# Second expert matrix of a hybrid-attention MoE backbone: loaded by partition halves in 8 KB runs instead of by column halves in 4 KB runs

## What is computed

```python
D_MODEL = 1024; N_GROUPS = 4; EXPERTS_PER_GROUP = 8      # 32 experts
TOP_K = 2; D_EXPERT = 256
# moe_w1, moe_w3: (DEPTH, 32, 1024, 256)    moe_w2: (DEPTH, 32, 256, 1024)

def hierarchical_moe(t, wg, bg, we, be, w1, w3, w2):
    ...                     # top-1 group, top-2 experts in it: combine (n, 32)
    def add_expert(acc, p):
        w1_e, w3_e, w2_e, c_e = p
        hidden = jax.nn.silu(t @ w1_e) * (t @ w3_e)
        return acc + c_e[:, None] * (hidden @ w2_e), None
    y, _ = lax.scan(add_expert, jnp.zeros_like(t), (w1, w3, w2, combine.T.astype(t.dtype)))
    return y
```

## Time and profile before

| what | value |
|---|---|
| time, median of 3 runs | 1144.73 us (1143.92 to 1146.38) |
| the profiled execution's own time | 1142.64 us |
| its span, first to last instruction | 1140.6 us |
| TensorE matmul busy | 976.4 us (86%) |
| VectorE, ScalarE, GpSimd busy | 29%, 23%, 21% |
| expert stage of layer 0 on TensorE, U and Dn | 365.2 to 635.3 us |
| expert stage of layer 1 on TensorE, U and Dn | about 858 to 1116.7 us |
| mean granted TensorE clock | 0.938 of 2.4 GHz |
| moved by DMA | 312.66 MB, mean 274 GB/s |

### The profile page before, as it was taken

The page is one execution under the profiler, slowest core; times in us unless marked ns, Lnnn a source line. Parts: engine busy times, 40 slices in busy tenths (PEclk is TensorE's granted clock), DMA queues, the critical chain, the costliest instruction groups (busy, mean ns, idle before and its releaser), DMA issues.

```text
span 1140.6 us, 17923 instructions
## 1 busy us (share of the span) xinstructions
PE 976.4 (86%) x5993; PEld 640.8 (56%) x5994; DVE 333.8 (29%) x720; ACT 259.5 (23%) x539; POOL 235.7 (21%) x331
## 2 busy tenths in 40 slices
PE   3999998989996998888998399999959989878881
PEld 2444475457884555555555175878845555555550
DVE  2169953542165110000100361255170101000103
ACT  3111023452131221111221230223122212111212
POOL 1118010100123132323231100000123323223310
PEclk9999999999997998998998799999978989998986
DMA  9992235994259799999999793232054999999972
GB/s 370 289 315 74 74 88 207 380 352 184 74 175 342 262 402 406 408 408 406 356 408 400 268 348 114 74 111 89 23 203 151 399 404 387 409 405 405 403 281 111
DMA packets 126899, 312.66 MB, mean 274 GB/s; under 512 B 28567, under 2 KB 59543, under 8 KB 126068
## 3 DMA queue, kind: packets, MB, share of 16 engines
q1 hardware_dynamic: 101488, 285.63, 66.5%
q10 hardware_dynamic: 14628, 13.53, 3.8%
q0 software_dynamic: 10720, 12.64, 3.2%
HBM read 312.49 MB, written 21.76 MB: 293 GB/s over the span
## 4 chain that ended last, share of the span: by engine, by line
PE 59%; DMA 26%; DVE 6%; ACT 3%; SPq 2%; issue 2%; ACTq 1%; POOL 0%; POOLq 0%; DVEq 0%
DMA ring<-in_moe_w 22%; PE ps L700 17%; PE ps L814 12%; PE ps L840 5%; PE ps L710 5%; PE ps L1005 4%; PE ps L636 3%; PE ps L1130 2%; SPq L572 2%; PE ps L667 1%; DMA PR<-in_odd_conv 1%; PE ps L792 1%; PE ps L683 1%; PE ps L729 1%; DMA RT<-pair_out 1%
## 5 line engine op out<-in xcount | busy, mean ns | idle before, releaser
L814 PE MATMUL ps<-ring,RT 128*64 128x256 f32 x2144 | 280.8, 420 | 59.7 <-DMA ring<-in_moe_w 56.7
L814 PEld LDWEIGHTS ps<-ring,RT 128*64 128x64 f32 x2144 | 186.1, 152 | 132.3 <-issue 68.2
L700 PE MATMUL ps<-RT,ring 128*128 128x512 f32 (+1 forms) x576 | 196.1, 500 | 1.0 <-ACT RT L1382 1.0
L700 PEld LDWEIGHTS ps<-RT,ring 128*128 128x128 f32 x576 | 109.4, 192 | 84.9 <-issue 76.6
L840 PE MATMUL ps<-ring,RT 128*64 128x512 f32 x536 | 127.8, 593 | 1.9 <-DVE RT L1771 1.1
L1754 DVE TENSOR_TENSOR RT<-RT,ps 64x256 f32<-64x256 f32 x64 | 27.0, 423 | 337.8 <-ACT RT L1332 337.8
L1332 ACT ACTIVATE RT<-ps 64x256 f32<-64x256 f32 x64 | 24.2, 378 | 300.1 <-PE ps L814 300.1
L1831 DVE SCALAR_TENSOR_TENSOR RAB<-RM,chan,RAB 128x512 f32<-128x512 f32 x120 | 79.7, 746 | 0.0
L2073 POOL DMA_INDIRECT RH<-hrow,sidx_all x64 | 67.5, 1055 | 55.8 <-POOL sidx_all L2070 55.8
L2085 POOL DMA_INDIRECT pair_out<-RH,sidx_all x64 | 65.3, 1021 | 59.0 <-POOL sidx_all L2082 54.7
L2050 POOL TENSOR_TENSOR X<-X,PR 128x512 f32<-128x512 f32 x12 | 15.2, 1266 | 270.8 <-DVE PR L1639 270.8
(11 more groups left out here) (229 smaller groups left out, 938.1 us busy)
## 6 DMA issues: line engine op xcount, KB each, us to landing
ring<-in_moe_w SPq DMA_DIRECT2D x384, 512.0 KB, 13.4
ring<-in_w_mod SPq DMA_DIRECT2D x96, 512.0 KB, 9.0
ring<-in_odd_w_in SPq DMA_DIRECT2D x24, 512.0 KB, 9.0
ring<-in_even_w_in SPq DMA_DIRECT2D x20, 512.0 KB, 10.2
ring<-in_even_w_out SPq DMA_DIRECT2D x8, 512.0 KB, 11.9
RT<-pair_out ACTq DMA_DIRECT2D x4, 1024.0 KB, 5.9
ring<-in_odd_w_out SPq DMA_DIRECT2D x8, 512.0 KB, 9.5
hrow<-RH ACTq DMA_DIRECT2D x6, 512.0 KB, 8.3
```

What stands on the lines that cost most here:

```text
L700: mm = pe.matmul(bank, w[:, c, P * ft:P * (ft + 1)], moving[:, c, :], start=(c == 0), stop=(c == NCH - 1))
L814: mm = pe.matmul(bank[CAP * k:CAP * (k + 1), 0:BLK], xt(c), w[k][:, BLK * c:BLK * (c + 1)], start=(c == 0), stop=(c == NCH - 1))
```

## The change

Only the two transfers that fill a slot with w2 change. The destination of a transfer was all 128 partitions and half of the slot's columns (4 KB in each); it is now 64 partitions and the whole width of the slot (8 KB in each): a = 0 fills partitions 0 to 63, a = 1 partitions 64 to 127. The source was every second row of the matrix; it is now a contiguous half of it, and each partition takes its two rows 2p and 2p+1 as one run of 8 KB. Number of transfers, bytes, semaphores, waits, and where each number lies in the slot at the end are as before. w1 and w3 keep their transfers; the diff only moves their destination into the branch.

```diff
@@ -566,11 +566,12 @@
                             w = A[name][l, bass.ds(i * PER_LOOP + q, 1), :, :]
                             for a in (0, 1):
                                 if k < 2:
+                                    dst = ring[:, n % RING, 1024 * a:1024 * (a + 1)]
                                     src = w[:, 512 * a:512 * (a + 1), :].rearrange("e (p j) n -> p (e j n)", j=4)
                                 else:
-                                    src = w.rearrange("e (p f) n -> p f (e n)", p=P)[:, a, :]
-                                sp.dma_start(ring[:, n % RING, 1024 * a:1024 * (a + 1)],
-                                             src).then_inc(landed[n % RING], 16)
+                                    dst = ring[64 * a:64 * (a + 1), n % RING, :]
+                                    src = w.rearrange("e (p f) n -> p (e f n)", p=P)[64 * a:64 * (a + 1), :]
+                                sp.dma_start(dst, src).then_inc(landed[n % RING], 16)
                 slots_filled[0] += 3 * EXPERTS
```

## The result

The changed kernel takes 1468.1 us (median of 4 runs, 1456.88 to 1475.62), before 1144.56 us in the same comparison: 1.28 times as long, 95% interval 1.273 to 1.290. The sign of the forecast was right, the size was not: 1273.5 us forecast, range to 1290. The profiled execution took 1475.6 us, its span 1473.6 us.

A forecast was written before the change was run, and what follows sets the result against it. The prediction took DMA loading of expert weights as the bound. 55 x 2.43 - 4.8 = 128.8 us on 1142.6 gave 1271.4 us profiled; with 2.1 us for the median, 1273.5 us, range 1140 to 1290.

The forecast's parts named there:

- What bounds the kernel: In both expert stages the DMA engines' loading of expert weights sets the pace, 8.73 and 8.25 us per expert.
- Sign, mechanism and own price: Change slower, chance 0.76; in w2 loads two engines share what each had alone, +2.43 us per expert.
- The weak row: Position-bias loads, the only ones to 64 partitions, with 256 B runs; best 0.2 us slice 179 GB/s, below half of 407.
- half of the partitions at a time: Each w2 transfer writes only 64 partitions; bounds no cost to +2.58 us per expert, taken as +2.43 us.
- B: Rival of partial sharing in w2 loads: engines out of step, half the price, 1206 us (1150 to 1255); chance 0.16.
- How many pay: Experts whose longer w2 load delays the end: 27 in layer 0, 28 in layer 1, less 4.8 us.
- Nothing is added there: Outside the expert loads, loads behind the experts start relative to their end as before; no added time.
- Rival C: In w2 loads only packets matter; longer runs gain 0.071 us per expert, 3.9 us less, 1140.8 us; chance 0.14.
- D: Rival of no difference in w2 loads: halves run side by side or long runs are cut again, 1144.7 us; chance 0.10.
- case A: Full sharing in w2 loads, or eight engines per half in turn: +2.1 to +2.7 us per expert, 1255 to 1288; chance 0.60.

The follow-up runs named there:

- experiment 6: Loads-only kernel, groups of 12 experts behind 0, 1, 4, 8 and 8 small transfers; w2 by partition halves in groups 1 to 4, which ran at 265 to 314 GB/s.

## Why the prediction was wrong

- **What bounds the kernel.** Right. Everything the DMA engines lost in the expert stages went to the end, and SP's issues, TensorE's clock and the tails cost nothing. The waits of U for weights came to 303.2 us, not 150 to 180. One reading was off without harm: the U of 5.36 us that the prediction puts at the lower clock had a mean granted clock of 0.68, so it ran at that level only in part.
- **Sign, mechanism and own price.** Right: w2 by itself runs at 217 instead of 407 GB/s, 4.83 us against 2.58, so +2.26 us. I took +2.43. The weak row, 179 GB/s in the earlier trace rows, pointed the right way, but at 256 B runs it could not have given the size.
- **The step that failed** is "half of the partitions at a time": I priced it as a term of w2 alone, +2.43 us per expert, and set its upper bound at both halves of w2 at half rate. What w1, w3 and the gathers would lose beside half transfers stood at nothing, without a reason. The runs showed 7.1 us per expert in layer 0 and 6.2 in layer 1: 2.3 us are w2's own, the other 4.8 and 3.9 are lost by what is in flight beside it. I also wrote that it did not matter whether the engines are in step; by the ends of the groups in experiment 6 it matters more than the term itself. The bound should have been the whole stream at half rate, 8.73 us more per expert, 55 x 8.73 = 480 us; the 333 us of the profiled execution lie inside it., where the engines run dry over 10 us, told that they are out of step; I used it only for a rival that makes the change cheaper (B), not for one that makes it dearer.
- **The account.** The 7.1 us of layer 0 come from the slowest of the change's four runs; in the versions with 4 KB halves and with layer 0 alone the same 14 steps took 14.4 and 14.6 us each, so 5.7 and 5.9 more than before. 5.2 are there without the gathers' bytes, and loads alone can reach the same 5.2. So 2.3 us are w2's own rate, some 2.9 the loss of w1 and w3 beside it, and the gathers add between 0.5 and 1.9. Mixed loads alone ran anywhere between 244 and 314 GB/s, so no single figure stands for the middle term, and its size could not have been told from the trace of the kernel before.
- **How many pay.** Too many by about a tenth. Layer 0's stage grew by 167 us (first Dn 387.20 to last 811.36, against 376.25 to 633.34), layer 1's by 154 us (1047.61 to 1447.74, against 868.43 to 1114.76). At 7.1 and 6.2 us that is the price of 24 and 25 experts, where 27 and 28 less 4.8 us were counted.
- **"Nothing is added there"** for the rest: wrong by some 6.5 us, for the small loads of ScalarE ahead of layer 0 meet the ring's filling, and their issue is held up. In two other versions (layer 0 alone, all by halves) the first Dn came 29 and 36 us late.
- **Rival C**, longer runs: its price was right, 3.1 to 4.7 us measured for 3.9, but under the larger loss. **D** is out, and so is **B**: both halves in turn are only 5% better than one, 217 against 207 GB/s. The second half of case A, eight engines at a time one after the other, was not needed: both halves in turn stay at 217 GB/s with all engines busy (DMA share 1.02).

## What to carry to other kernels

Before a large load is cut by partitions, look at which partitions each transfer covers: a transfer to one neighbouring half runs at about half the rate, every second partition or all 128 at the full one, and longer runs give their small gain there. A slow pattern in a shared queue is not an item with a price of its own. Bound it by the whole stream at the slow rate, and if the pattern cannot be avoided, fewer transfers in flight can be faster.

## What was not expected of the hardware

- One third of the bytes in half-partition transfers took the stream from 407 down to between 224 and 232 GB/s, lower than all three matrices that way (240 and 247 GB/s from 450 to 540 and from 540 to 600 us of that kernel, whose stages were also 40 and 19 us shorter; two other versions with the mixture reached 239 and 243 in layer 0):

```profile
450.00:540.00 90.00, 54.39 (x298) 32.72 (x296) 4.29 (x13) 9.79 (x19) 14.71 (x24) 0.73 1.03 240
540.00:600.00 60.00, 37.07 (x196) 22.23 (x192) 3.57 (x10) 7.46 (x14) 11.23 (x19) 0.77 1.03 247
```

- An added wait per slot was worth 167 us.
- The same list of transfers ran at 265 to 314 GB/s, and the slow streams are those whose engines finish far apart.
